# Hybrid decoder step on one core: first loads on three queues, and VectorE's work at the decode loop's start in another order

## What is computed

```python
h = jnp.einsum('bld,de->ble', x, w_in_l)                 # x: 512 + 64 rows of 1024, w_in: 1024 x 5200
qa, fa, ia, ga, qb, kb, vb, gb, qi, ki, wi = jnp.split(h, IN_OFFSETS, axis=-1)
o_a, s_new = hgrn2_branch(qa, fa, ia, ga, lb_l, norm_g_l, s0)
q, k, v, qi, ki, wi = dsa_inputs(qb, kb, vb, qi, ki, wi, pos, kn_g_l, kn_b_l)   # rotary; LayerNorm of ki
o_b = attend(q, k, v, qi, ki, wi)                        # decode: all cached indexer keys are scored,
x_new = merge_and_norm(x, o_a, o_b, gb, w_out_l, ln_g_l, ln_b_l)   # the best 256 attended to
```

## Time and profile before

| | |
|---|---|
| median of three runs | 785.72 us (784.81 to 791.41) |
| the profiled execution | 787.79 us, its span from the first to the last instruction 786.1 us |
| mean granted TensorE clock | 0.968 of full speed |
| PE busy | 734.3 us, 93% of the span |
| DVE, ACT, POOL busy | 491.0 us, 265.0 us, 238.1 us |
| moved by DMA | 114.68 MB, 146 GB/s over the span |

### The profile page before, as it was taken

How to read it: one execution, slowest core, us unless ns; L and a number is a source line. 1 busy time by engine, 2 the same in 40 slices (tenths; PEclk the granted TensorE clock), 3 DMA queues, 4 the chain that set the end, 5 groups by cost and what they waited for, 6 DMA issues and landing times. The chain is left out here.

```text
span 786.1 us, 13385 instructions
## 1 busy us (share of the span) xinstructions
PE 734.3 (93%) x4554; PEld 433.9 (55%) x4554; DVE 491.0 (62%) x923; ACT 265.0 (34%) x571; POOL 238.1 (30%) x342
## 2 busy tenths in 40 slices
PE   4688999999999899999999999999999997989994
PEld 3344444544444455767655566774477774864441
DVE  0213399999999546545555645555489985294535
ACT  3104710235665122223223222226556444340000
POOL 2610013046987223222222222221143461450000
PEclk9899999999999899999999999999999996699998
DMA  9900063060400588988888899861040000510611
GB/s 229 376 17 1 4 212 115 1 220 1 167 1 0 161 252 257 348 262 282 290 253 256 257 306 310 279 191 43 14 200 2 1 1 0 159 70 0 199 55 41
DMA packets 61316, 114.68 MB, mean 146 GB/s; under 512 B 8370, under 2 KB 21763, under 8 KB 61251
## 3 DMA queue, kind: packets, MB, share of 16 engines
q1 hardware_dynamic: 31122, 52.28, 21.7%
q0 software_dynamic: 12448, 40.27, 15.1%
q10 hardware_dynamic: 17680, 21.30, 8.1%
HBM read 106.60 MB, written 7.23 MB: 145 GB/s over the span
## 5 line engine op out<-in xcount | busy, mean ns | idle before, releaser
L473 PE MATMUL banks<-wbuf,xT 128*128 128x512 f32 (+1 forms) x448 | 147.4, 533 | 5.5 <-DMA wbuf<-in_w_in 5.5
L338 POOL DMA_DIRECT2D arena<-in_cache_v x128 | 70.0, 547 | 205.3 <-issue 205.3
L473 PEld LDWEIGHTS banks<-wbuf,xT 128*128 128x128 f32 (+1 forms) x448 | 65.8, 176 | 81.1 <-issue 70.8
L733 PE MATMUL banks<-wbuf,xT 128*128 128x512 f32 (+1 forms) x288 | 101.2, 531 | 0.0
L1262 DVE TENSOR_REDUCE small<-banks 128x1 f32<-128x512 f32 x32 | 22.1, 692 | 98.6 <-PE banks L664 98.6
L1220 DVE MAX8 small<-arena 64x8 f32<-64x2112 f32 x32 | 75.1, 2348 | 1.3
L1222 DVE MATCH_REPLACE8 arena<-small,arena 64x2112 f32<-64x2112 f32 x32 | 74.7, 2334 | 0.0
L647 PE MATMUL banks<-ident,arena 128*128 128x128 f32 x512 | 69.0, 278 | 4.1 <-DVE wbuf L1255 3.8
L647 PEld LDWEIGHTS banks<-ident,arena 128*128 128x128 f32 x512 | 57.1, 142 | 25.7 <-issue 19.3
L719 PE MATMUL banks<-xT,arena 128*128 128x288 f32 x256 | 67.4, 406 | 0.0
L1028 ACT COPY wbuf<-banks 128x512 f32<-128x512 f32 x64 | 37.2, 582 | 75.8 <-PE banks L647 69.8
(11 more groups left out here) (256 smaller groups left out, 1139.7 us busy)
## 6 DMA issues: line engine op xcount, KB each, us to landing
arena<-in_cache_k SPq DMA_DIRECT2D x128, 256.0 KB, 3.4
arena<-in_cache_v POOLq DMA_DIRECT2D x128, 256.0 KB, 3.8
wbuf<-in_w_in ACTq DMA_DIRECT2D x8, 2048.0 KB, 12.8
arena<-in_w_in ACTq DMA_DIRECT2D x8, 512.0 KB, 6.0
arena<-in_x_prompt SPq DMA_DIRECT2D x8, 256.0 KB, 6.0
wbuf<-in_w_out SPq DMA_DIRECT2D x1, 2048.0 KB, 9.0
xT<-in_w_out SPq DMA_DIRECT2D x1, 2048.0 KB, 13.7
arena<-in_x_prompt SPq DMA_DIRECT2D x4, 512.0 KB, 8.4
```

The lines of the kernel that those rows point to most:

```text
L338: e.dma_start(buf[n % 2][:, i, :], cache[bass.ds(pg, 1), 0].rearrange("a p h d -> p (a h d)")).then_inc(arrived[n % 2], 16)
L473: mm = pe.matmul(psum[a * NS:a * NS + ROWS[t], n % PB, 0:w // split], xT[:, c, t * P:t * P + ROWS[t]], wbuf[:, WB[g], c, a * w // split:(a ...
L733: mm = pe.matmul(psum[a * NS:a * NS + ROWS[t], bank, 0:512 // split], xT[:, c, t * P:t * P + ROWS[t]], wbuf[:, WB[g], c, a * 512 // split: ...
```

## The change

The first loads are issued by three engines. SP keeps `pages`, the left halves of the five x tiles, and all that followed. ACT issues, ahead of everything else, `ident`, the right halves of x tiles 0 and 1, the key weights (now into `w_k`, a place of their own and with a semaphore of their own, `wk_in`), the right halves of tiles 2 to 4, and groups 1 and 2. POOL issues `gather`, `table` and `ofseq`. The gathers wait for group 1 instead of tile 3 of x. `ident` counts with `pages` (`pages_in`, 32).

On DVE the work ahead of the decode loop moves into it: the query block (`decode_queries`) behind the first `keys_out`, the rest (`rest_of_queries`) behind the second, the lower bound (`lower_bound`) to pass 16. ACT's wait for `banks_ok` moves to its first use.

```diff
@@ -200,6 +200,7 @@
         newbias = carve(NS)[0:NS]
         SP = {b: bias_p[:, POFF[b]:POFF[b] + (b + 1) * P] for b in (1, 2, 3)}
         kiwi_f = relu_s[0][0:80, 0:TOK]
+        w_k = relu_s[0][:, 640:1280].rearrange("p (c n) -> p c n", c=KC)
...
-        bias_ok, sp_ok, lbl_ok = sem("bias_ok"), sem("sp_ok"), sem("lbl_ok")
+        bias_ok, sp_ok = sem("bias_ok"), sem("sp_ok")
-        table_in, rows_ok = sem("table_in"), sem("rows_ok")
+        table_in, rows_ok, wk_in = sem("table_in"), sem("rows_ok"), sem("wk_in")
...
-        WCOUNT = (1, 1, 2, 2, 3, 3, 4, 5, 6)
+        WCOUNT = (0, 1, 1, 2, 2, 3, 3, 4, 5)
-        NCONST = 6 * 16
+        NCONST = 5 * 16
...
+        def load_x_half(e, h, which):
+
+            w = slice(h * W2, (h + 1) * W2)
+            for t in which:
+                e.dma_start(xin[0:ROWS[t], t, w], (xp_rows[t] if t < NT else xs_rows)[:, w]
+                            ).then_inc(x_half[h] if t == 0 else x_in[t], 16)
+
         with nc.Block() as block:
             @block.sync
             def _(sp):
                 sp.dma_start(pages[:], page_table.rearrange("s g -> (s g)").rearrange("(a n) -> a n", a=1)).then_inc(pages_in, 16)
-                sp.dma_start(ident[:], c_ident).then_inc(const_in, 16)
-                sp.dma_start(gather[:], c_gather).then_inc(table_in, 16)
-                sp.dma_start(table, page_table.rearrange("s g -> (s g)").partition_broadcast(P)).then_inc(table_in, 16)
-                for t in range(NT + 1):
-                    src = xp_rows[t] if t < NT else xs_rows
-                    for h in range(2):
-                        w = slice(h * W2, (h + 1) * W2)
-                        sp.dma_start(xin[0:ROWS[t], t, w], src[:, w]).then_inc(x_half[h] if t == 0 else x_in[t], 16)
-
+                load_x_half(sp, 0, range(NT + 1))
                 sp.dma_start(gki[:, 0, :], idx_norm_g.partition_broadcast(P)).then_inc(ki_par_in, 16)
                 sp.dma_start(gki[:, 1, :], idx_norm_b.partition_broadcast(P)).then_inc(ki_par_in, 16)
                 sp.dma_start(rope[:], c_rope).then_inc(ki_par_in, 16)
...
-                sp.wait_ge(pages_in, 16)
+                sp.wait_ge(pages_in, 32)
@@ -480,7 +480,7 @@
 
             @block.tensor
             def _(pe):
-                pe.wait_ge(const_in, 16)
+                pe.wait_ge(pages_in, 32)
...
-                    pe.wait_ge(w_got[0], 16)
+                    pe.wait_ge(wk_in, 16)
                     for a in range(2):
                         for c in range(KC):
-                            mm = pe.matmul(psum[0:80, a, 0:HALF], wbuf[:, 0, c, 0:80], xT[:, c, a * HALF:(a + 1) * HALF],
+                            mm = pe.matmul(psum[0:80, a, 0:HALF], w_k[:, c, :], xT[:, c, a * HALF:(a + 1) * HALF],
@@ -901,10 +901,13 @@
 
             @block.scalar
             def _(act):
-                load_w(act, 0)
+                act.dma_start(ident[:], c_ident).then_inc(pages_in, 16)
+                load_x_half(act, 1, range(0, 2))
+                act.dma_start(w_k, w_rows[:, :, G_KI:G_KI + 80]).then_inc(wk_in, 16)
+                load_x_half(act, 1, range(2, NT + 1))
+                load_w(act, 1)
+                load_w(act, 2)
                 for n in range(2 * (NT + 1)):
-                    if n == 4:
-                        load_w(act, 1)
...
-                load_w(act, 2)
...
-                act.wait_ge(lbl_ok, 1)
+                act.wait_ge(lb_ok, 1)
                     if s:
                         act.wait_ge(p_tr, 5 * s)
+                    else:
+                        act.wait_ge(banks_ok, 4)
                     nc.scalar.activation(probs_n[:, 0:NS], psum[:, MB, M_S], ACT.Exp, bias=nmx[s % 2][:, 4:5],
                                          accum_out=sums[s % 2][:, 4:5]).then_inc(ex, 1)
...
-                act.wait_ge(banks_ok, 4)
                 me.link(nc.vector.tensor_tensor(lb, lbl[:, 0], lbl[:, 1], ALU.max))
-                nc.vector.tensor_tensor(lbt, lbl, lb.unsqueeze(1).to_broadcast([P, 2, HA]), ALU.subtract).then_inc(lbl_ok, 1)
+                nc.vector.tensor_tensor(lbt, lbl, lb.unsqueeze(1).to_broadcast([P, 2, HA]), ALU.subtract).then_inc(lb_ok, 1)
-                dve.wait_ge(lb_ok, 1)
-                me.link(nc.vector.tensor_tensor(lbc, lbt[:, 0], lbt[:, 1], ALU.add))
...
-                nc.vector.memset(psum[:, MB, :], 0.0).then_inc(banks_ok, 1)
-                dve.wait_ge(pacc, 3 * HI)
-                dve.wait_ge(roped, ROPED_Q[NT - 1])
-                dve.wait_ge(stored, STORES)
-
-                nc.vector.memset(probs_n, 0.0).then_inc(banks_ok, 1)
-                nc.vector.memset(v_tok[NS:P, NT, :], 0.0).then_inc(banks_ok, 1)
...
 
+                def lower_bound():
+
+                    dve.wait_ge(lb_ok, 2)
+                    me.link(nc.vector.tensor_tensor(lbc, lbt[:, 0], lbt[:, 1], ALU.add))
+                    me.link(nc.vector.reciprocal(lbc, lbc))
+                    me.link(nc.vector.tensor_tensor(lb, lbt[:, 0], lbc, ALU.mult))
+                    me.link(nc.vector.tensor_scalar(lbc, lb, -1.0, 1.0, ALU.mult, ALU.add))
+
+                def decode_queries():
+
+                    me.link(nc.vector.memset(qbd, 0.0))
+                    dve.wait_ge(tr2_act, TURN_NO["q", NT] + 1)
+                    for h in range(2):
+                        nc.vector.tensor_copy(
+                            qbd_v[DH * h:DH * h + DH, :, :, NNEW * h:NNEW * h + NNEW],
+                            qT[DH * h:DH * h + DH, :, SEQ:TOK].rearrange("p j (s q) -> p s j q", s=NSEQ)).then_inc(qbd_ok, 1)
+
+                def rest_of_queries():
+
+                    for t in (2, 3):
+                        turned_out(dve, nc.vector.tensor_copy, tr2_dve, ("q", t), SB0 + 1 + t)
+                    dve.wait_ge(tr2_dve, 2)
+                    nc.vector.memset(psum[:, OB, :], 0.0).then_inc(banks_ok, 1)
+                    nc.vector.memset(psum[:, MB, :], 0.0).then_inc(banks_ok, 1)
+
+                    nc.vector.memset(probs_n, 0.0).then_inc(banks_ok, 1)
+                    nc.vector.memset(v_tok[NS:P, NT, :], 0.0).then_inc(banks_ok, 1)
+
                 base = 2 * (TOPK_S // 8) + 1
 
                 def strike(k):
+                dve.wait_ge(pacc, 3 * HI)
+                dve.wait_ge(roped, ROPED_Q[NT - 1])
+                dve.wait_ge(stored, STORES)
                 for n in range(NG + 1):
                     s, g = n // 4, n % 4
                     more = n < NG
                     apart = g == 1 and s > 0
                     if more:
                         keys_out(n, 0)
+                    if n == 0:
+                        decode_queries()
                     if apart:
                         gather_out(s - 1)
                     elif more:
@@ -1331,6 +1344,8 @@
                         keys_out(n, 2)
                         if apart:
                             strike(3 * n)
+                        if n == 0:
+                            rest_of_queries()
                         strike(3 * n + 1)
                     if g == 0 and s:
                         shares(s - 1)
+                    if n == NG // 2:
+                        lower_bound()
@@ -1479,9 +1496,11 @@
             @block.gpsimd
             def _(pool):
                 me = Tally(pool, pool_own)
+                pool.dma_start(gather[:], c_gather).then_inc(table_in, 16)
+                pool.dma_start(table, page_table.rearrange("s g -> (s g)").partition_broadcast(P)).then_inc(table_in, 16)
                 pool.dma_start(ofseq[:], c_ofseq).then_inc(ofseq_in, 16)
                 pool.wait_ge(rows_ok, 1)
-                pool.wait_ge(x_in[NT - 1], 32)
+                pool.wait_ge(w_got[1], 16)
                 for s in range(NSEQ):
                     for o in range(2):
                         pool.indirect_dma_start(
```

13 lines of the change are left out of this document (removed).

## The result

In the first comparison the changed kernel took 777.13 us, median of four executions (776.89 to 782.75), beside 788.06 us of the kernel before (four, 784.81 to 791.41): a ratio of 0.989, 95% interval 0.985 to 0.993, or 8.7 us. The prediction said 773. The profiled execution took 776.89 us, 10.9 less than that of before.

The account below looks back on a forecast made before the run. PE, busy for 734.3 of 786.1 us, was taken as the bound, time being won in its waits and low clock. Start 6.7 plus decode loop 5.8 gave 12.5 us, from 785.7 to 773 us, range 767 to 779.

Parts of the forecast that it names:

- The waits: PE's 5.5 us wait for group 1's weights and 3.8 us wait for DVE's copy of turned keys would go.
- First transposes: At the start, PE's first transposes would come at 5.9 us, between 5 and 8.45, for 8.45 before.
- ACT held: At the start, full queues hold ACT until 10.5 us (9 to 13.5); its first copy comes at 11.9 us.
- L504: The key product would begin at 17.9 us, 6.0 us of work after ACT's first copy; 16.65 us before.
- EARLY's begin and its clock: EARLY would begin at 27.0 us, 4.2 us earlier, and save 2.5 us more by having no low clock.
- Group 1 and 2: Weights: group 1 lands at 21.8 us (19 to 25), group 2 at about 33 us, both before their use.
- L532 released by POOL: Sign of a wrong forecast: POOL's gathers and rotations, expected to end at 46.6 us, release PE's L532, needed at 51.2 us.
- Everything behind L532 follows one another, so both gains last to the end: From L532 on, scores, search and loop are sequential, so the gains of 6.7 and 5.8 us last to the end.
- The decode loop: At the loop's start, 3.84 us idle and 2.9 us of low clock go, 0.9 us comes back: net 5.8 us.
- The sum: Start 6.7 us plus decode loop 5.8 us gives 12.5 us, from 785.7 us to 773 us.
- a longer hold: Rival, chance 0.14: at the start ACT is released at 13.5 us, EARLY begins at 30.0; 9.5 us gained, 776.2 us.
- The slower rival: Chance 0.03: gathers wait for group 1; landing after 26.4 us costs time, at 47 us over 1% slower (793.8 us).

Follow-up runs that it names:

- the repeats: The changed kernel, unchanged, run three more times beside the kernel before, ten executions each: ratios 1.000, 0.996 and 1.000.
- e3_release: The changed kernel with the load of group 2 moved behind ACT's ten copies of x: 788 us, ratio 1.001.
- e2_loop: The kernel before with the decode loop's part of the change alone: 780.18 us beside 787.07, ratio 0.991.
- r1_after: The changed kernel again, unchanged, beside the kernel before: 787.46 us, ratio 1.000.
- e2_again: The kernel before with the decode loop's part of the change alone, measured a second time: ratio 0.993.
- e1_start: The kernel before with the start's part of the change alone: 793.45 us, ratio 1.008.
- e17_records: The kernel before with the decode loop's part, plus 120 memsets of 128x2 on DVE beside EARLY: ratio 0.995.

## Why the prediction was right or wrong, step by step

- *The waits.* Right: both waits of the earlier trace rows went, and PE's wait for x stayed about as long.
- *First transposes.* 5.48 us, forecast 5.9; 4.7 to 5.5 in the repeats.
- *ACT held.* Right: released at 10.7 us (10.9 to 11.3 in the repeats), forecast 10.5; first copy at 12.0, forecast 11.9. The hold was spread over several issues (2.0 us for the right half of the fourth tile of x, 1.0 for the next, 3.3 for group 2) and did not fall on group 2's alone. Wrong was that it decides the size: e3_release took it away and L504 came no earlier.
- *L504.* Wrong: 19.7 us for 17.9. The step "from ACT's first copy to L504 the work itself takes 6.0 us" failed. PE waited another 0.86 us for x, whose last right halves stand behind the key weights and beside SP's constants, and the work itself was slower. PE's 40 transposes (L494) took 421 ns each in the median, as in all three repeats (417 to 421), against 273 before; 421 ns is also what the transposes of L647 took in before's stretch at 0.52, and 273 ns at 1.00 (the views print 1.00 for the start in both traces, so here the durations must tell the pace). The last 24 took 4.63 us; before's last 16 took 1.09 us for eight full and 0.71 us for eight small ones, by which these 24 would have taken 2.9 us (an estimate). Repeats gave 18.1, 18.9 and 20.6. The rule of the Trainium skill, "DMA: Bandwidth & Descriptors", section "Issuing engines are not separate DMA queues", weighed in the prediction, agrees with these traces: 217 GB/s over the first 12 us, 221 before.
- *EARLY's begin and its clock.* EARLY at 28.7 for 27.0 (27.1 to 29.5 in the repeats), so 2.5 us instead of 4.2; the low clock's 2.5 us were right, 23.73 less 21.24.
- *Group 1 and 2.* Group 1 landed at 24.8 us (POOL's first gather starts at 25.6), 3.0 us later than forecast, still in time; group 2 at about 31.
- *L532 released by POOL.* Did not happen; DVE's 2.0 us as before.
- *"Everything behind L532 follows one another, so both gains last to the end".* This is the step that failed in the first result. The start's 6.7 us were 5.0 at L532 and only 0.7 at the loop's start, since the clock fell behind L532: 10.2 us at half clock cost 4.0 to 4.3 us in the two traces that have it, against the three that have none (200.5 to 204.4 and 204.8 us, above). The sum had the low clock only where it would go away, and no term for one that comes. That this fall comes and goes between executions is shown (e2_loop has it, r1_after has not), what decides it isn't.
- *The decode loop.* Right, and a little small: PE's second turn of keys leads by 7.5 us, of which 0.7 came from before, so 6.8 for 5.8. The 0.9 us that I had come back did not: DVE's maximum began at 263.17 us, not at 264.3, and PE at L684 (264.71 us) waited for nothing. Alone the part gave 7.3 and 5.9 us by its two ratios.
- *The sum.* 12.5 forecast, 8.7 measured first: the start's term is the mis-sized one. By e2_loop and e2_again 5.9 to 7.3 of the 8.7 us are the loop's, so that the start was worth 1 to 3 us by the ratios and 0.7 us in the trace, for 6.7 forecast, and -6 us alone in e1_start. The last 3.6 us of the profiled pair's 10.9 came from a shorter low stretch about 650 us (17.1 us at half clock for 27.3), which no step had, and which differs between executions of one kernel. That the first time came within 4 us of the forecast is so in part luck, and that it lies near the 776.2 of the rival "a longer hold" is luck altogether: ACT was released at 10.7 us, not 13.5.
- *What was missing altogether, and made the change worth nothing in the repeats.* The prediction saw in the gathers' later start only POOL's chain and group 1's arrival, and costed PE's wait for group 1 as loss alone. It had no term for PE's losing 7 to 10 us in EARLY under the gathers. The trace of before gave no warning: there PE ran L504 (16.65 to 24.6 us) at 1.00 beside 352 GB/s, and EARLY from 36.3 to 40.9 us at 1.00 while the last gathers moved (323 GB/s), both without a gap. The slower rival named the gathers, but by the wrong mechanism.

Open is what holds PE and its signals in the gaps; why the first result's profiled execution had none, with the same order and the gathers at the same time, though the repeats' three traces had them (it also lost none of its landings, which they did); and whether its other three were clean too, which only their times suggest.

## What to carry to other kernels

A wait that a change removes may be paying for something: look at what else moves in the time into which the work is pulled, here 4.2 MB of gathers over a dense run of short matmuls. Measure the halves of a change apart, and in more than one comparison: here one half gave 6 to 7 us in both of its own (4 us with e17_records' memsets; the intervals overlap), and the other took them back in nearly every execution. A low clock that one trace shows gone can come back elsewhere in the next. When an engine stands with no releaser, look at whether the engines that wait for it were released on time, and whether the profile is complete there, before you settle on a cause.
